# Experts sorted by load into 32 straight-line slots of fixed width, in a hybrid attention, S5 and mixture-of-experts layer

## What is computed

```python
def _moe(hn, w_router, b_router, w1, b1, w2, b2):   # hn: 1024 tokens x 1024
    logits = xt @ w_router + b_router               # 32 experts
    top_val, top_idx = lax.top_k(logits, 4)
    gates = jax.nn.softmax(top_val, axis=-1)
    # for each expert e, on the tokens that chose it:
    hb = xb @ w1[e] + b1[e]                         # 1024 -> 2048
    x_glu = jnp.minimum(hb[:, :1024], 7.0)
    x_lin = jnp.clip(hb[:, 1024:], -7.0, 7.0)
    act = x_glu * jax.nn.sigmoid(1.702 * x_glu) * (x_lin + 1.0)
    out = act @ w2[e] + b2[e]                       # 1024 -> 1024
    # y[token] += gate * out, over its four experts
```

## Time and profile before

| | us |
|---|---|
| median of 3 runs (3651.44 to 3652.81) | 3652.19 |
| the profiled execution, its span | 3656.0 |
| expert stage, 1120 to 3610 | 2490.0 |
| PE busy in the whole span | 2743.1 |
| DVE, ACT, POOL busy | 765.6, 451.8, 448.4 |

### The profile page before, as it was taken

How to read it: one execution, slowest core, us unless ns; L and a number is a source line. 1 busy time by engine, 2 the same in 40 slices (tenths; PEclk the granted TensorE clock), 3 DMA queues, 4 the chain that set the end, 5 groups by cost and what they waited for, 6 DMA issues and landing times. The chain is left out here.

```text
span 3656.0 us, 43499 instructions
## 1 busy us (share of the span) xinstructions
PE 2743.1 (75%) x16220; PEld 2288.0 (63%) x16221; DVE 765.6 (21%) x1850; ACT 451.8 (12%) x938; POOL 448.4 (12%) x952
## 2 busy tenths in 40 slices
PE   8997999999877565776567755777686877568664
PEld 4455777654437565666567755777686777568654
DVE  1003222222453121111111111121121111111212
ACT  2002222211310000000000100001010001000001
POOL 6502860000010000000000000000000000000001
PEclk9997555799988787888788877888788888789877
DMA  5116000400064465364556755566576655644553
GB/s 147 43 46 152 1 1 0 150 23 23 1 243 154 128 199 165 107 201 153 160 157 197 242 170 158 186 196 210 176 234 213 204 174 185 200 157 146 167 161 111
DMA packets 470806, 524.79 MB, mean 144 GB/s; under 512 B 33027, under 2 KB 439811, under 8 KB 470188
## 3 DMA queue, kind: packets, MB, share of 16 engines
q1 hardware_dynamic: 455328, 473.39, 38.9%
q0 software_dynamic: 13536, 41.96, 5.3%
q10 hardware_dynamic: 1324, 0.81, 0.1%
HBM read 479.93 MB, written 48.24 MB: 144 GB/s over the span
## 5 line engine op out<-in xcount | busy, mean ns | idle before, releaser
L1650 PE MATMUL ps<-xT,we 128*128 128x128 f32 (+7 forms) x8192 | 1075.9, 296 | 0.0
L1650 PEld LDWEIGHTS ps<-xT,we 128*128 128x128 f32 x8192 | 1068.7, 198 | 6.7
L1665 PE MATMUL ps<-ident,xg 128*128 128x128 f32 x368 | 95.2, 430 | 760.6 <-issue 759.5
L1665 PEld LDWEIGHTS ps<-ident,xg 128*128 128x128 f32 x368 | 67.6, 219 | 783.4 <-issue 774.2
L1650 PE MATMUL ps<-act,we 128*128 128x128 f32 (+7 forms) x4096 | 520.5, 289 | 0.0
L1650 PEld LDWEIGHTS ps<-act,we 128*128 128x128 f32 x4096 | 513.6, 191 | 3.3
L1755 DVE TENSOR_SCALAR glu<-ps,b1T 128x128 f32<-128x128 f32 (+1 forms) x256 | 104.7, 409 | 764.2 <-PE ps L1650 764.2
L1775 DVE TENSOR_SCALAR xT<-ps,g_moe 128x128 f32<-128x128 f32 (+1 forms) x128 | 44.8, 404 | 814.8 <-PE ps L1665 814.8
L1580 POOL DMA_INDIRECT acc_dram<-orow,sx x48 | 76.3, 1589 | 1046.7 <-ACT orow L1818 1037.0
L1834 ACT ACTIVATE sg<-glu 128x256 f32<-128x256 f32 (+1 forms) x128 | 65.3, 510 | 1055.9 <-DVE glu L1755 1055.9
L1784 DVE TENSOR_SCALAR outT<-ps,b2T 128x128 f32<-128x128 f32 (+1 forms) x256 | 104.6, 409 | 409.4 <-PE ps L1650 407.2
(11 more groups left out here) (294 smaller groups left out, 2186.1 us busy)
## 6 DMA issues: line engine op xcount, KB each, us to landing
we<-in_w SPq DMA_DIRECT2D x384, 1024.0 KB, 7.3
wa<-in_w_in SPq DMA_DIRECT2D x4, 2048.0 KB, 10.3
skew_dram<-line_dram SPq DMA_DIRECT2D x8, 576.0 KB, 9.6
xrow<-in_x SPq DMA_DIRECT2D x8, 512.0 KB, 5.8
wa<-in_w_xkv SPq DMA_DIRECT2D x2, 2048.0 KB, 8.1
bias<-skew_dram SPq DMA_DIRECT2D x8, 512.0 KB, 6.1
wd<-in_w_out SPq DMA_DIRECT2D x4, 1024.0 KB, 13.0
h<-in_x SPq DMA_DIRECT2D x1, 4096.0 KB, 17.4
```

Source lines behind the costliest of these rows:

```text
L1650: last = nc.tensor.matmul(out, m.we[s][:, k, (j % 2) * P:(j % 2 + 1) * P], moving[:, k, 0:W], start=(k == 0), stop=(k == KC - 1))
L1665: last = nc.tensor.transpose(m.ps[:, q % 2, width * i + P * half:width * i + P * half + P], (m.xg0, m.xg1)[half][:, k * P:(k + 1) * P], m. ...
```

## The change

The experts are sorted by load and run in 32 slots, the fullest first. Slot s is written out as straight-line code on each engine, for a fixed width: 14 wide slots of 256 to 132 columns and 18 narrow ones of 128.

- `phase_e`: after the counts are known, DVE forms count x 32 + (31 - expert), sorts these 32 keys with four `max` and three `match_replace`, and recovers the expert of each slot in `slot_e`. SP's first twelve weight loads wait for this (`sorted_ok`) and read the expert from a register. POOL makes a few more constants.
- Wide slots compute as before, at their own width. The first layer has four PSUM banks, the second two (before: three each), and banks 6 and 7 are kept for transposes. The copies use exactly the slot's width. The next slot's rows are transposed between the layers (`x_in(s + 1)` behind the last first-layer group); the results of the slot before are transposed after groups 1 and 3 of the first layer.
- Narrow slots turn the operands round: the tokens (`xT`, then `actT`) are stationary and weights move, 512 columns at a time, in both layers. Biases enter as products with rows of ones ahead of the sums. Activations have tokens on partitions, so they are transposed for the second layer (`act_in`), and the results need no transposes.
- Weights go through 14 buffers of 1 MB in a ring. POOL copies index, gate and bias columns of a slot by register, two slots ahead.
- Tokens of an expert beyond its slot's width are left to a loop at the end, which runs only if a flag (`need_any`) says so.

The core of the diff:

```diff
-WIDTHS = tuple(range(P, WIN + 1, STEP))
-L1S, SLOTS = 8, 12
+SLOT_WIDTH = (256, 224, 200, 168, 164, 164, 160, 160, 160, 156, 144, 136, 136, 132) + (P,) * 18
+PIECES, RING = 12, 14
...
-        ch.link(v.tensor_copy(m.cnt_i[:], m.pref[0:1, NB, :]))
-        ch.link(v.tensor_scalar(m.cnt_i[:, 0:1], m.pref[0:1, NB, 0:1], 1.0, None, ALU.max))
+        ch.link(v.scalar_tensor_tensor(out=key[0], in0=m.pref[0:1, NB, :], scalar=float(E), in1=m.rev[:], op0=ALU.mult, op1=ALU.add))
+        for r in range(4):
+            top = m.ranked[:, 8 * r:8 * r + 8]
+            ch.link(v.max(top, key[r % 2]))
+            if r < 3:
+                ch.link(v.match_replace(key[(r + 1) % 2], top, key[r % 2], -1.0))
+        ch.link(v.tensor_copy(m.slot_i[:], m.ranked[:]))
+        v.tensor_scalar(m.slot_e[:], m.slot_i[:], E - 1, E - 1, ALU.bitwise_and, ALU.bitwise_xor).then_inc(sorted_ok, 1)
...
+        for s in range(E):
+            reg = regs[s % 2]
+            sp.reg_load(reg, m.slot_e[0:1, s:s + 1])
+            e = sp.snap(reg, min_val=0, max_val=E - 1)
...
+                if n >= RING:
+                    piece_used(sp, n - RING)
+                load_piece(sp, m, a, s, i, e)
...
+        for s in range(E):
+            if s + 1 < E:
+                gather(s + 1)
+            if s:
+                scatter(s - 1)
+            if s + 2 < E:
+                columns(s + 2)
...
+        def put(emit):
+            n = group[0]
+            if n >= 2:
+                t_copied(pe, n - 2)
+            emit(t_bank(n)).then_inc(t_full, 1)
+            group[0] += 1
...
+        def narrow(s):
+            for r in range(4):
+                k = 2 if r >= 2 else 1
+                last = nc.tensor.matmul(m.ps[:, r, :], m.ones[32 * r:32 * r + k, :], m.brow[32 * r:32 * r + k, s % 2, :],
+                                        start=True, stop=False, skip_group_check=True)
...
+                        for k in range(4):
+                            last = nc.tensor.matmul(m.ps[:, 2 * part + c, :], m.xT[:, 4 * half + k, 0:P], view[:, k, :], start=False,
+                                                    stop=(half == 1 and k == 3), skip_group_check=True)
...
+        def broad(s):
...
+                if j in (1, 3) and s and wide[s - 1]:
+                    rows_out(s - 1, j // 2)
+            if s + 1 < E:
+                x_in(s + 1)
...
+            for j in range(2, KC):
+                pe.wait_ge(l2_dve, l2_dve_before[s] + j - 1)
+                second(j, range(KC))
...
+        for s in range(E):
+            (broad if wide[s] else narrow)(s)
+        flag = pe.alloc_register("more_pe")
+        pe.wait_ge(need_ok, 4)
+        pe.reg_load(flag, m.need_any[0:1, 0:1])
+        with pe.If(pe.snap(flag, min_val=0, max_val=1) > 0):
...
-        v.memset(m.ps[:, 2:8, :], 0.0).then_inc(psum_init, 1)
-        for buf in (m.outT, m.orow0, m.orow1):
-            v.memset(buf[:], 0.0).then_inc(psum_init, 1)
+        v.memset(m.outT[:], 0.0).then_inc(init_f, 1)
+        v.memset(m.brow[:], 1.0).then_inc(init_f, 1)
+        v.memset(m.crow[:], 0.0).then_inc(init_f, 1)
...
+            for p in range(4):
+                front(2 * p)
+                if p:
+                    back(p - 1)
+                front(2 * p + 1)
+            back(3)
...
+                C, col = broad(s)
+                if s + 1 < E:
+                    x_out(s + 1)
+                second(s, C, col)
```

More of the change, by code:

```diff
@@ L1546, in _ @@
     @block.sync
     def _(sp):
[L1548 to L1559, removed]
+        regs = [sp.alloc_register("expert_sp0"), sp.alloc_register("expert_sp1")]
@@ new lines, in gather @@
+        def gather(s):
+            for half in range(tiles_of[s]):
+                q, rows = tile0[s] + half, P if half == 0 else rest[s]
+                if q >= 2:
+                    pool.wait_ge(t_full, taken[q - 2])
+                pool.wait_ge(idx_ok, 3 * s + 1)
+                pool.indirect_dma_start(xg[q % 2][0:rows, :], None, a.xn_dram, bass.IndirectOffsetOnAxis(m.gx[0:rows, s % 3, half:half + 1], 0),
+                                        bounds_check=last_token, oob_is_err=False).then_inc(gathered[q % 2], 16)
@@ new lines, in _ @@
+        pool.wait_ge(init_f, 4)
+        columns(0)
+        gather(0)
+        columns(1)
+        for s in range(E):
[5 more added lines that the diff above has]
+                columns(s + 2)
+        scatter(E - 1)
+        for q in (tile0[E] - 1, tile0[E] - 2):
+            pool.wait_ge(scattered[q % 2], 16 * (q // 2 + 1))
+        flag = pool.alloc_register("more_pool")
+        pool.wait_ge(need_ok, 4)
@@ new lines, in rows_out, with emit, x_ready @@
+        def rows_out(s, half):
+            if half == 0:
+                pe.wait_ge(l2_dve, l2_dve_before[s + 1])
+            for quarter in range(2):
+                def emit(out):
+                    for i in range(4):
+                        last = nc.tensor.transpose(out[:, P * i:P * i + P], m.outT[:, 4 * quarter + i, half * P:half * P + P], m.ident[:])
+                    return last
+                put(emit)
+        def x_ready(s):
+            for half in range(tiles_of[s]):
+                for quarter in range(2):
+                    t_copied(pe, at[("X", s, half, quarter)])
@@ new lines, in _ @@
+        link(v.scalar_tensor_tensor(out=m.lim[:], in0=start, scalar=float(P), in1=width, op0=ALU.add, op1=ALU.is_gt))
+        link(v.tensor_tensor(m.over[:], m.over[:], m.lim[:], ALU.mult))
+        v.tensor_copy(m.need[:], m.over[:].rearrange("p e w -> p (e w)")).then_inc(need_ok, 1)
+        v.reduce_max(m.need_any[:], m.over[:].rearrange("p e w -> p (e w)"), AX.X).then_inc(need_ok, 1)
+        x_out(0)
+        for s in range(E):
+            if wide[s]:
+                C, col = broad(s)
+                if s + 1 < E:
+                    x_out(s + 1)
+                second(s, C, col)
+            else:
+                narrow(s)
+                if s + 1 < E:
+                    x_out(s + 1)
```

825 lines of the change are left out of this document (553 added, 272 removed).

## The result

The changed kernel takes 2871.73 us (median of 5 runs, 2839.98 to 2874.49) against 3652.19 us for the kernel before (median of 5 runs, 3598.84 to 3653.82). The ratio is 0.787, 95% interval 0.7803 to 0.7937. The forecast was 2933 us with a range of 2895 to 3015.

The account below looks back on a forecast made before the run. The expert stage was taken as bound by PE plus loop jumps, DMA not full. Start 1134.6, wide slots 877, narrow slots 880, end 17.2 and final stage 27.4 sum to 2936 us span, 2933 as median, range 2895 to 3015.

Parts of the forecast that it names:

- Rival 3: Expert stage: the gaps stay because jumps aren't their cause; 3676 us if all 743 us come back; chance 0.03.
- Rival 4: Spill loop at the end: an extra window runs after all, 82 us, so 3015 us or more; chance 0.03.
- (a): Wide slots: transposes of results, 16 a slot at 0.122 us each, 27.3 us.
- (b): Wide slots: transposes of the next slot's rows, now between the two layers, 26.4 us.
- (c): Wide slots, between layers: third group of row transposes waits for DVE's copy, 2.6 us a slot, 34 us; bounds 0 and 4.1.
- (e): Wide slots: matmuls at half clock after a gap, 1.9 us per cold start; 10 us taken, between 2 and 27.
- Rival 5: Wide slots: every stretch of transposes and waiting between layers goes cold, 27 us in place of 10, 2950 us; chance 0.12.
- (d): Wide slots, second layer: two banks instead of three, third group waits for a copy, 0.3 us a slot, 4 us.
- Rival 1: Narrow slots: bias products let the clock fall, at most 95 us; 2981 us for half, 3028 for all; chance 0.13.
- Rival 2: Narrow slots: weight loads at 235 GB/s limit PE, 53.5 us a slot, 83 us more, 3016 us; chance 0.07.
- Rival 6: Narrow slots: PE stays at half clock as in attention, doubling 880 us, 3813 us, slower than before; chance 0.02.
- Start: Before the expert stage: sorting, memsets and gathers put the rows at 1128.7 us and the first matmul at 1134.6 us.

Follow-up runs that it names:

- b_straight: Kernel before with its expert stage as straight-line code on all engines, the drawn inputs' loads built in: median 2822.38 us, stage time 1659.2 us.
- b_twowidths: Kernel before with the tree of widths cut to 128 and 256 columns: 3712.19 us, stage time 2537.1 us.
- a_far: Changed kernel with a flag read and a never-met condition skipping 512 matmuls behind each slot on TensorE: 2940.32 us, stage time 1764.6 us.
- b_pestraight: Kernel before with only TensorE's program written out straight, the other engines keeping their loops: 3210.75 us, stage time 2039.7 us.
- a_splitx: Changed kernel with the second half of the next wide slot's row transposes moved into the middle of the second layer: median 2827.68 us, stage time 1652.9 us.
- a_allwide: Changed kernel with 17 of the 18 narrow slots run as wide ones of 132 columns: 2957.61 us, stage time 1780.1 us.
- a_onegroup: Changed kernel with all bias products of narrow slots reading partitions 0 and 1 instead of 0, 32, 64 and 96: 2958.75 us, stage time 1784.8 us.
- a_fullrows: Changed kernel with each bias product of narrow slots done over all 128 rows by a selector of ones and zeros: 2926.01 us, stage time 1747.6 us.
- a_jump2048: Changed kernel with a never-true condition around 2048 register moves behind each slot on TensorE, of which nothing shows in the trace: 2868.45 us, stage time 1695.1 us.
- a_near: Changed kernel with a flag read and a never-met condition skipping 2 matmuls behind each slot on TensorE: 2802.23 us, stage time 1694.8 us.

## Why the prediction was right, and where it was wrong

**What bounds the kernel, and that the gaps go: right.** The earlier trace rows gave the cause, and b_straight and b_twowidths showed it, with the same 2.8 us for each instruction read in a gap. It is no price for every read: in a_far the reads behind narrow slots cost nothing. Rival 3 is out. What the reading missed is that the other engines' loops alone would have kept 381 of the 819 us (b_pestraight). That cost nothing here, because the change straightens every engine.

**Loads and spill: right.** There is no product behind slot 32, and the slots come as 14 wide, then 18 narrow. Rival 4 is out.

**Wide slots: 862.3 us (1103.82 to 1966.15), forecast 877.** (a), (b): eight transposes take 0.87 us from start to start, 0.109 each and not 0.122, which gives 6 us; 1.8 more fell into the first narrow slot. The mean that I used came from groups of 12 with their end time in it. (c): 13 waits of 2.18 to 3.01 us, 31.6 in sum, against 34. That was the order of DVE's work, read from the diff:

```profile
1165.02 1.45 PE L1790 MATMUL ps<-ident,xg 128*128 128x128 f32 x8 [3.01 <-DVE xT L1987]
...
1449.17 1.94 PE L1790 MATMUL ps<-ident,xg 128*128 128x128 f32 x8 [2.37 <-DVE xT L1987]
1450.90 18.92 PE L1903 MATMUL ps<-actT,we 128*128 128x164 f32 x128
...
1631.07 1.06 PE L1790 MATMUL ps<-ident,xg 128*128 128x128 f32 x8 [2.35 <-DVE xT L1987]
1631.97 17.83 PE L1903 MATMUL ps<-actT,we 128*128 128x160 f32 x128
```

(e): 5 of the 13 stretches restart cold, as the middle pair of these shows, and 8 don't, as the last pair shows after the same idle time. The cost is 8 us in the second layers and 3 in the transposes, and the stage's own cold start, which the term includes, is another 1.8 (57.32 us for the first layer of the first slot, at 0.50 to begin with; 55.49 in a_splitx, at 1.00): 13 against 10. Rival 5 would have all 13 cold; this trace has both outcomes. The prediction named beside it the Trainium skill, TensorE: Matmul & The Clock Gate, section PE-mode transpose, by which transposes don't count as PE-busy the same way. The same transposes stand in all 13 stretches, so the trace does not bear out that such a stretch goes cold each time; it does not refute the page's statement either. In a_allwide a 132-column slot does restart cold. Why one stretch holds its clock and the next doesn't is open. (d): PE waits for no bank of the second layer (idle before L1903: 0.3 us in all), so those 4 us didn't come. The last 4 us of the 15 lie in how products and transposes were counted. The line goes through durations, and a duration reaches some 0.16 us past the start of what follows (57.32 us, but 57.16 from start to start).

**Narrow slots: 828.4 us (1966.15 to 2794.58), forecast 880. This is the step that failed.** Products, transposes and the half microsecond for the second activation group came as worked out. The term that was mis-sized is the bias rows: I took 12 x 0.430 = 5.2 us, "rows don't shorten it", with 5.2 and 10.3 as bounds. Measured are 1.07 + 1.06 = 2.13 us, 3.03 less, 55 us over 18 slots. a_onegroup and a_fullrows show that the sentence itself is true for products one behind the other, and what it left out: the diff puts the four products at partitions 0, 32, 64 and 96, and on four groups they run side by side. The price came from a shape that fills 64 rows and shows nothing of this. The working had a bound above and none below, although an operation that the trace doesn't show should have had both. A low bound, an estimate from the earlier trace rows, of four products in the time of one, and two in the time of one (0.86 + 0.86 = 1.72 us a slot), lies 3.5 us below what I took, 63 us over 18 slots. The range would have begun at 2832 and held the result.

**Rival 1** (the clock falls in narrow slots) didn't happen: 1.00 over all of them. a_onegroup shows that it was no idle thought: a restart costs 1.5 us a slot where the few-row products follow each other. **Rival 2** (feeding) is out: 279 GB/s were moved, above the 235 of the earlier trace rows, and PE never waits for a weight. **Rival 6** is out with rival 1.

**Start: right but for the attention stage.** The first matmul follows the first transposes by 5.8 us (forecast 5.9). That the stage begins at 1098 us in this execution and not at 1128.7 is the clock in attention, told above. One sum in that part was off: 12.58 MB at 383 GB/s from 1074.4 on end at 1107 and not 1114, and neither is later than their use. The end of the stage's last product to the span's end is 43.6 us, forecast 44.6; in it stand ACT's last copy, the last scatter (issued at 2795.59) and the reads that follow (from 2810.70).

**The sum.** Narrow slots -52, wide slots -15, end -1; against that +6, since I set the median 3.8 us below the span and it lies 2 above that of its own execution. Together -62, and measured -61. This takes the start of the stage as forecast; the median execution was not profiled, but a_jump2048, with the same stage, starts it at 1127.64 and takes 2868.45 us.

## What to carry to other kernels

Idle time with the releaser "issue" ahead of the same line each time is the path through the loop: count the instruction reads in it, compare with straight-line code, and look whether the other engines' loops are nearly as long before straightening only one. The reads alone don't give the price: 35 more of them beside the long products of the narrow slots cost nothing. Before a new layout is credited with a gain, set it against the old one without its jumps. An operation that the trace lacks needs a low bound as well as a high one, and its price hangs on where its operands lie, since products on different groups of 32 partitions go side by side. In straight-line code a wait of 2 to 3 us can cost up to 2 us more in a cold restart, so it pays to move the waited-for half behind other work.

## What the runs showed of the hardware that I had not expected

- Four bias products (eight instructions) of 512 columns take 1.07 us from start to start on four partition groups and 3.68 us on one; two products take 1.06 and 1.9.
- One- and two-row products one behind the other are followed by a granted clock of 0.50, those of 128 rows, which last as long (3.60 us), are not: the 48 instructions behind them take 22.3 to 22.6 and 20.76 us.
- A skipped block of 512 matmuls makes two more instruction reads. It costs 4.9 us behind each of the 14 wide slots and nothing behind the narrow ones; a skipped block of 2 costs nothing that shows.
- Attention, with PE busy for 379 to 383 of 400 us, was granted 0.57, 0.67 and 0.77 in three executions of the same code (before, after, a_near), and the expert stage started at 1127, 1098 and 1061 us. Nothing in these runs tells why.
